# Opening of the first block: modulation rows in pairs with two projection chunks tile by tile, and the input's products with its root on VectorE

## The reference

```python
mod = jax.nn.silu(c) @ ada_w[0] + ada_b[0]                    # 6 * 1024 numbers
sh_a, sc_a, g_a, sh_f, sc_f, g_f = jnp.split(mod[:, None, :], 6, axis=-1)
h = rms_norm(x, attn_norm[0]) * (1.0 + sc_a) + sh_a           # 256 x 1024
y = sparse_mixer(h, ...)     # begins with h @ sp_w_in: 1024 x (3*512 + 512 + 768 + 24)
x = x + g_a * y
```

## Time and profile before

| | |
|---|---|
| median of 3 runs | 2203.2 us (2202.68 to 2203.76) |
| profiled execution, its own time | 2204.52 us |
| span of the profiled execution | 2202.7 us |
| granted TensorE clock, mean over the span | 0.996 of full |
| PE busy | 2156.7 us (98%) |
| DVE busy | 1847.5 us (84%) |
| ACT busy | 1327.0 us (60%) |
| HBM read | 630.13 MB, 287 GB/s over the span |

### The profile page before, as it was taken

How to read it: one execution, slowest core, us unless ns; L and a number is a source line. 1 busy time by engine, 2 the same in 40 slices (tenths; PEclk the granted TensorE clock), 3 DMA queues, 4 the chain that set the end, 5 groups by cost and what they waited for, 6 DMA issues and landing times.

```text
span 2202.7 us, 31747 instructions
## 1 busy us (share of the span) xinstructions
PE 2156.7 (98%) x12960; PEld 1899.7 (86%) x12960; DVE 1847.5 (84%) x2321; ACT 1327.0 (60%) x1495; POOL 112.2 (5%) x155
## 2 busy tenths in 40 slices
PE   6999999999999999999999999999999999999998
PEld 4888999889999979999888888888888888888886
DVE  7967888876998677888896988989897988989896
ACT  3574433575343776434633777777777777777775
POOL 3000111000010000100000000000000000000021
PEclk9999999999999999999999999999999999999999
DMA  9855988625887616885643899999998999999992
GB/s 370 299 190 201 344 314 316 230 77 211 305 299 276 225 39 239 325 325 179 227 171 136 325 372 370 365 345 363 370 358 343 369 365 371 368 345 357 373 360 85
DMA packets 137360, 633.30 MB, mean 288 GB/s; under 512 B 9304, under 2 KB 21625, under 8 KB 115194
## 3 DMA queue, kind: packets, MB, share of 16 engines
q1 hardware_dynamic: 112698, 536.83, 64.9%
q0 software_dynamic: 24512, 94.38, 11.4%
HBM read 630.13 MB, written 1.05 MB: 287 GB/s over the span
## 4 chain that ended last, share of the span: by engine, by line
PE 82%; DVE 12%; DMA 3%; issue 2%; ACT 1%; SPq 0%; DVEq 0%; ACTq 0%
PE ps L1266 80%; DVE wring_rounded L3211 3%; DMA aring<-in_ada_rows 3%; DVE aring L3238 2%; DVE work L3211 1%; PE ps L2391 1%; DVE OT L3235 1%; PE ps L1469 1%; DVE F L3218 1%; DVE F L3211 0%; PE ps L1444 0%; DVE work L3750 0%; ACT scr_rounded L2472 0%; ACT F_rounded L2472 0%; DVE work_rounded L3211 0%
## 5 line engine op out<-in xcount | busy, mean ns | idle before, releaser
L3211 DVE TENSOR_TENSOR wring_rounded<-wring,scr_rounded 128x2048 fp32r<-128x2048 f32 (+1 forms) x314 | 569.6, 1845 | 58.2 <-ACT scr_rounded L2472 57.8
L2472 ACT ACTIVATE scr_rounded<-wring 128x2048 fp32r<-128x2048 f32 (+1 forms) x314 | 479.7, 1553 | 181.8 <-PE ps L1266 125.3
L1266 PE MATMUL ps<-wring_rounded,OT_rounded 128*128 128x512 f32 (+1 forms) x1184 | 314.8, 390 | 2.6 <-DVE wring_rounded L3211 1.7
L1266 PEld LDWEIGHTS ps<-wring_rounded,OT_rounded 128*128 128x128 f32 x1184 | 220.1, 188 | 47.2 <-DVE wring_rounded L3211 2.3
L3238 DVE CUSTOM_DVE_ANT_0 aring<-aring,F,vec 128x1024 f32<-128x1024 f32 x152 | 187.9, 1283 | 35.6 <-DMA aring<-in_ada_rows 34.8
L3211 DVE TENSOR_TENSOR wring_rounded<-wring,H_rounded 128x2048 fp32r<-128x2048 f32 (+1 forms) x85 | 193.9, 2281 | 24.2 <-ACT H_rounded L2472 24.0
L3211 DVE TENSOR_TENSOR wring_rounded<-wring,aring_rounded 128x2048 fp32r<-128x2048 f32 x84 | 193.4, 2302 | 12.4 <-ACT aring_rounded L2472 12.1
L2472 ACT ACTIVATE H_rounded<-wring 128x2048 fp32r<-128x2048 f32 (+1 forms) x85 | 162.3, 1910 | 54.7 <-issue 38.4
L2472 ACT ACTIVATE aring_rounded<-wring 128x2048 fp32r<-128x2048 f32 x84 | 161.2, 1919 | 54.4 <-PE ps L1266 54.4
L1266 PE MATMUL ps<-V_rounded,wring_rounded 128*128 128x256 f32 x1184 | 177.9, 285 | 4.6 <-DVE wring_rounded L3211 4.6
L1266 PE MATMUL ps<-work_rounded,F_rounded 128*128 128x256 f32 x1056 | 169.8, 283 | 0.0
(11 more groups left out here) (391 smaller groups left out, 3695.8 us busy)
## 6 DMA issues: line engine op xcount, KB each, us to landing
wring<-in_moe_gate SPq DMA_DIRECT2D x56, 2048.0 KB, 8.5
wring<-in_moe_up SPq DMA_DIRECT2D x56, 2048.0 KB, 9.0
wring<-in_moe_down SPq DMA_DIRECT2D x56, 2048.0 KB, 8.6
aring<-in_ada_rows POOLq DMA_DIRECT2D x88, 1024.0 KB, 7.5
wring<-in_ffn_w_gate SPq DMA_DIRECT2D x10, 2048.0 KB, 11.0
wring<-in_ffn_w_up SPq DMA_DIRECT2D x10, 2048.0 KB, 15.3
wring<-in_ffn_w_down SPq DMA_DIRECT2D x10, 2048.0 KB, 10.5
wring<-in_diff_w_in SPq DMA_DIRECT2D x6, 2048.0 KB, 15.3
```

The costliest lines, as they stand in the source:

```text
L1266: return pe.matmul(dst, lhsT, rhs, start=start, stop=stop, **kw)
L2472: return act.activation(dst, src, ACT.Copy, **kw)
L3211: return ve.tensor_tensor(dst, x, y, op)
```

## The change

- The modulation rows are loaded by pairs: load k has the 128 rows of the shift for tile k and the 128 rows of the scale for the same tile. `vec`, the tables and X come ahead of them. Between load k and k+1 stand tile k of the chunks 2048:2560 and 1536:2048, 256 KB each. Load 6 goes to a buffer that load 0 had and waits for it.
- DVE makes X * root as a product of its own (`root_tile`; the root is first copied from PSUM by ACT), and ACT multiplies by gsc and adds the shift, twice: once rounded to `OTupper`, once to H. DVE then subtracts the one from the other (`lower_tile`) and makes the rests of two weight slices per tile (`slice_rest`).
- PE multiplies tile by tile for both chunks at once, with six empty products ahead of each tile (12 matmuls of 512 columns a tile, 96 in all), in the banks 0, 1, 4 and 5.
- The order behind it is 2560, 0, 512, 1024; the queries of the first two chunks are rotated and turned first. `add_more(0)` and (1) stand where (2) and (3) stood, and (2) to (5) at the end. The chunk 0:512 now has the banks 6 and 7, which `hid_job` and `kvc_job` use after it.

The diff, cut to its core; in the parts of ACT and DVE behind the opening, lines taken out are not shown.

```diff
-        sp_w = [Chunk(ring) for _ in range(5)]
+        sp_w = [Chunk(ring, dmas=0 if j < 2 else 1) for j in range(5)]
...
-        sp_tok = [[J(2 * (j % 2) + qt) for qt in range(2)] for j in range(6)]
+        sp_tok = [[J(b + qt) for qt in range(2)] for b in (0, 4, 2, 6, 0, 2)]
...
+            o = ((n + 1) % 2 if n < DF_PARTS else n % 2) * 2048
+            return buf[:, o:o + 2048]
...
+            first_rows = a["ada_rows"][0, 0:2 * D, :].rearrange("(s t p) k -> p t s k", s=2, p=P)
+            w = a["sp_w_in"][0]
...
+                if n == 6:
+                    sp.wait_ge(ada_used, 1)
+                sp.dma_start(ada0_buffer(n), first_rows[:, n]).then_inc(ada0_loaded[n], 16)
+            def load_slices(k, loaded):
+                for j, lo in enumerate((2048, 1536)):
+                    sp.dma_start(slice_weights(j, k, False), w[k * P:(k + 1) * P, lo:lo + CH]).then_inc(loaded, 16)
+            sp.dma_start(vec[:], a["vec"]).then_inc(vec_loaded, 16)
+            load_first(0)
+            for k in range(1, KT):
+                load_slices(k - 1, ada0_loaded[k])
+                load_first(k)
+            load_slices(KT - 1, last_slice_loaded)
...
-            for j, lo, n in ((1, 2560, 280), (2, 1536, 512), (3, 0, 512), (4, 512, 512)):
+            for j, lo, n in ((2, 2560, 280), (3, 0, 512), (4, 512, 512)):
...
-            pe.wait_ge(ada_used, 7)
-            idle_products(3, 14)
-            by_token_split(sp_w[0], 0, sp_tok[0], CH, OTupper, Hlower, HI_TILES[0])
+            idle_products(3, 12)
+            for job in sp_tok[0] + sp_tok[1]:
+                job.open(pe)
+            def slice_products(k):
+                def run(x, lower, last):
+                    for j in range(2):
+                        wk = slice_weights(j, k) if lower else slice_part(j, k)
+                        for qt, job in enumerate(sp_tok[j]):
+                            ins = mm(PS[job.b][:, :], x[:, k, qt * P:(qt + 1) * P], wk,
+                                     k == 0 and x is OTupper and not lower, last and k == KT - 1)
+                            if last and k == KT - 1:
+                                fill(job, ins)
+                    return ins
+                idle_products(3, 6)
+                pe.wait_ge(hi_tile, k + 1)
+                pe.wait_ge(slice_upper, 2 * k + 2)
+                run(OTupper, False, False)
+                pe.wait_ge(slice_lower, 2 * k + 2)
+                run(OTupper, True, False)
+                pe.wait_ge(lo_tile, k + 1)
+                ins = run(Hlower, False, True)
+                if k < KT - 1:
+                    ins.then_inc(slice_used, 1)
+            pe.sem_inc(part_used, 3)
+            for k in range(KT):
+                slice_products(k)
+            pe.sem_inc(part_used, 1)
             pe.wait_ge(con_loaded, 16)
-            by_token_split(sp_w[1], 2, sp_tok[1], 280, OTupper, Hlower)
-            by_token_split(sp_w[2], 4, sp_tok[2], CH, OTupper, Hlower, None, lambda: turn_rows(sp_turn[1], 2))
+            by_token_split(sp_w[2], 4, sp_tok[2], 280, OTupper, Hlower)
+            turn_rows(sp_turn[1], 0)
...
+            copy(rstd[:], PS[norm_spread[0].b][:, 0:T]).then_inc(norm_spread[0].bank.free, 1)
+            act.sem_inc(part_upper_made, 4)
+            def shifted_tile(k):
+                act.wait_ge(scaled, k + 1)
+                act.wait_ge(by_root, k + 1)
+                scale, shift = gsc[:, k:k + 1], mod[:, 0, k:k + 1]
+                affine(OTupper[:, k, :], H[:, k, :], scale, shift).then_inc(hi_tile, 1)
+                affine(H[:, k, :], H[:, k, :], scale, shift).then_inc(x_shifted, 1)
+            def round_slices(k):
+                slice_loaded(act, k)
+                if k >= 2:
+                    act.wait_ge(slice_used, k - 1)
+                for j in range(2):
+                    copy(slice_part(j, k), slice_weights(j, k, False)).then_inc(slice_upper, 1)
+            for k in range(KT):
+                shifted_tile(k)
+                round_slices(k)
+            round_part(sp_w[2], 4, 280)
             act.wait_ge(con_loaded, 16)
+            sp_tok[1][1].filled(act)
+            round_part(sp_w[2], 5, 280)
+            row_squares(sp_tok[1], 8)
+            row_roots(0, 8)
...
             row_squares(sp_tok[0], 8)
+            round_part(sp_w[3], 6)
             for qt, job in enumerate(sp_tok[0]):
+                sp_turn[1][qt].filled(act)
                 copy(work[:, 1152 + qt * 512:1280 + qt * 512], PS[job.b][:, P:2 * P])
                 copy(V[:, qt * 1024 + 512:qt * 1024 + 640], PS[job.b][:, 3 * P:4 * P])
+            row_roots(2, 8)
+            turned_rows(sp_turn[1], (F[:, 8:12, :], vc("nsa_q_rest")), (other_queries[:, 4:8, :], vc("nsa_q_rest", 1)))
+            round_part(sp_w[3], 7)
+            row_squares(sp_tok[2], 2)
+            for qt, job in enumerate(sp_tok[2]):
                 copy(V[:, qt * 1024 + 640:qt * 1024 + 768], PS[job.b][:, P:2 * P])
                 copy(gates[:, qt, :], PS[job.b][:, 256:280])
+            row_roots(4, 2)
+            round_part(sp_w[4], 8)
+            for qt, job in enumerate(sp_turn[2]):
                 job.filled(act)
                 for m, (t, k) in enumerate(((12, 0), (15, None), (13, 1), (14, 2))):
                     dst, src = F[:, t, qt * P:(qt + 1) * P], PS[job.b][:, m * P:(m + 1) * P]
                     last = copy(dst, src) if k is None else act.activation(dst, src, ACT.Identity, scale=vc("nsa_k_rest", k))
                 last.then_inc(job.bank.free, 1)
+            sp_turn[2][1].emptied(act)
             for par in range(2):
                 for g in range(2):
                     for half in range(2):
                         last = copy(*window(par, g, half, 1))
             last.then_inc(windows_ready, 1)
             row_squares(sp_tok[3], 8)
+            round_part(sp_w[4], 9)
             row_roots(6, 8)
+            round_part(sp_w[5], 10)
...
+                w, o = ada0_buffer(n), VEC["ada_b"][0] + n
+                for m in range(2):
+                    last = ve.tensor_tensor_reduce(w[:, m, :], w[:, m, :], crow, 1.0, vec[:, o + KT * m:o + KT * m + 1],
+                                                   ALU.mult, ALU.add, mod[:, 0, n + KT * m:n + KT * m + 1])
+                last.then_inc(ada_used, 1)
+            def root_tile(k):
+                tt(H[:, k, :], X[:, k, :], rstd[:], ALU.mult).then_inc(by_root, 1)
+            def scale_tile(k):
+                ve.wait_ge(ada_used, k + 1)
+                o = VEC["attn_norm"][0] + k
+                stt(gsc[:, k:k + 1], mod[:, 0, KT + k:KT + k + 1], 1.0, vec[:, o:o + 1], ALU.add, ALU.mult).then_inc(scaled, 1)
+            def slice_rest(j, k):
+                ve.wait_ge(slice_upper, 2 * k + j + 1)
+                tt(slice_weights(j, k), slice_weights(j, k, False), slice_part(j, k).bitcast(F32), ALU.subtract).then_inc(
+                    slice_lower, 1)
+            def lower_tile(k):
+                ve.wait_ge(x_shifted, k + 1)
+                tt(Hlower[:, k, :], H[:, k, :], OTupper[:, k, :].bitcast(F32), ALU.subtract).then_inc(lo_tile, 1)
...
+            ve.sem_inc(part_lower_made, 4)
+            for job in crow_job:
+                job.emptied(ve)
+            add_first(0)
+            scale_tile(0)
+            for k in range(1, KT):
+                add_first(k)
+                if k == 1:
+                    inverse(0)
+                    norm_spread[0].emptied(ve)
+                    root_tile(0)
+                scale_tile(k)
+                root_tile(k)
+                lower_tile(k - 1)
+                for j in range(2):
+                    slice_rest(j, k - 1)
+            lower_tile(KT - 1)
+            for j in range(2):
+                slice_rest(j, KT - 1)
+            part_rest(sp_w[2], 4, 280)
+            part_rest(sp_w[2], 5, 280)
             ve.wait_ge(rotary_made, 4)
             ve.wait_ge(con_loaded, 16)
+            row_sums(0, 8)
+            rows(0, sp_tok[1], 8, ((0, 0, 8, 4),), None)
             def rests(j):
                 for n in (2 * j + 3, 2 * j + 4):
                     if n < 12:
+                        part_rest(sp_w[n // 2], n)
+            row_sums(2, 8)
+            part_rest(sp_w[3], 6)
+            rows(2, sp_tok[0], 8, ((0, 0, 2, 5), (4, 4, 2, 6)), sp_turn[1])
+            part_rest(sp_w[3], 7)
+            row_sums(4, 2)
+            rows(4, sp_tok[2], 2, ((0, 6, 2, 7),), None)
+            part_rest(sp_w[4], 8)
+            sp_turn[2][1].emptied(ve)
...
-            add_more(2)
+            add_more(0)
...
-            add_more(3)
+            add_more(1)
...
-            for n in range(4, 6):
+            for n in range(2, 6):
```

More of the change, by code:

```diff
@@ L711, in build @@
         for M, tag in ((moe2, "again"),):
-            for name in ("upper", "lower", "gathered", "sel", "wsel", "xg", "st", "silu", "hid", "ht", "ye", "acc"):
+            for name in ("upper", "lower", "gathered", "sel", "wsel", "hid"):
                 M[name] = sem(f"{tag}_{name}")
```

(34 more changed lines are left out.)

77 lines of the change are left out of this document (16 added, 61 removed).

## The result

The changed kernel takes 2216.4 us (median of four runs, 2215.88 to 2219.15) against 2203.5 (2202.68 to 2204.01) for the kernel before beside it: 1.0062 times as long, interval 1.0044 to 1.0079. It is slower, by 13 us where I forecast 2.6, and outside my range. The profiled execution took 2215.88 us, its span 2214.0 against 2202.7.

A forecast was written before the change was run, and what follows sets the result against it. The prediction took the kernel to be bound by PE (82% of the chain), with DVE's late work deciding: compressed_scores at 124.1 against 121.55, so 2.6 us later, 2205.8 us against 2203.2. The range was 2200 to 2211.

The forecast's parts named there:

- The first pair: Opening: load 1 and the slices 0 end a queue of 4.3 MB and are usable at 15.2 us.
- DVE's beat: Opening's stream: DVE needs 4.6 us per tile against 3.9 for the loads, so it sets the pace.
- PE in the stream: Opening: PE needs 4.05 us a tile, is the later one at the last, and ends the stream at 55.9.
- DVE's list: From 57.1 us to the compressed keys' signal: 55.9 us of work plus 5.6 of waits, giving 118.6.
- The new wait: End of DVE's work before the signal: 3.1 us of waiting for the load of add_more(4).
- The sum: Signal at 118.6 plus 5.5 us puts compressed_scores at 124.1 against 121.55, so 2.6 us later; chance .64.
- The clock: Rival, in the opening's stream: waits drop PE to 1.2 GHz, 7.8 us a tile; three low tiles give about 2214; chance .11.
- PE's clock at 1.00 behind 24 us: Sign of a right forecast: in the trace after, PE's granted clock is full from 24 us on.
- a memset before 114, a stream's end past 59: Signs of a wrong forecast: DVE's memset before 114 us (then PE decides), or the opening's stream ending past 59.
- The faster one: Rival: stream follows the loads, ends at 51.9, late loads land in time; 4.6 us gained, 2198.6; chance .14.
- The third: Rival, opening's stream: loads at 300 GB/s take 5.2 us a tile, stream ends 4 us later, 2210; chance .11.
- PE's list alone: From 55.9 us to compressed_scores: PE by itself would get there at 120.9, a gain of .7 us.

The follow-up runs named there:

- warm_units: The changed kernel with 12 empty products on PE ahead of its wait for the compressed keys and 10 behind unit 2's scores: 2210.2 us, ratio 1.0036.
- before_moved_warm: The kernel before with its six additions moved late as in the change, plus 12 and 10 empty products on PE: 2207.7 us, ratio 1.0016.
- stream_no_empties: The changed kernel without the six empty products ahead of each tile in the opening's stream: 2211.6 us, ratio 1.0040.
- gaps_no_empties: The changed kernel with add_more(4) and (5) moved to units 1 and 3 and the stream's empty products left out: 2203.0 us, ratio 1.0003.
- adds_in_gaps: The changed kernel with add_more(4) and (5) moved ahead of the row maxima of units 1 and 3: 2205.6 us, ratio 1.0021.
- before_two_in_units: The kernel before with add_more(6) and (7) moved ahead of the row maxima of units 1 and 10: 2206.3 us, ratio 1.0009.
- before_adds_moved: The kernel before with only its six add_more moved to the places the change gives them: 2214.6 us, ratio 1.0045.
- product_with_scale: The changed kernel with DVE's product per tile taking the scale again and ACT adding only the shift: 2219.0 us, ratio 1.0064.
- adds_in_units: The changed kernel with add_more(4) and (5) moved ahead of the row maxima of units 3 and 4: 2210.4 us, ratio 1.0029.
- load_apart: The changed kernel with the second half of the output weights loaded only once add_more(3)'s load has landed: 2215.8 us, ratio 1.0053.

## Why the prediction was wrong

**The first pair, DVE's beat, PE in the stream: right.** 16.76 for 15.2, 4.48 for 4.6, 57.1 for 55.9. The 1.6 us at the start are the pair's own landing, which ends DVE's wait at 16.76. X was late too (PE's sums for the norm end at 17.8, not 15.0) but stayed covered by the two additions. The shorter beat gave back 0.7.

**DVE's list: right in kind, 3.2 us short.** The term that was too small is the wait for loads. DVE takes the list up at 58.55 for 57.1, which is 1.4. The new wait, which I saw in one place (3.1 us ahead of `add_more(4)`), is three: 1.42, 1.70 and 1.61, 4.73 in all. I had the load for (4) issued 0.3 behind (2) and landing 5.25 later; a load in that stretch takes 5.2 us alone and 10.5 beside 2 MB of weights. The work of 55.9 us was right within 1 us: from 58.55 to the memset's signal are 63.3 us, and the forecast 61.5 plus the 1.6 of waits is 63.1; the waits for ACT were 0.6 less than forecast, the work that much more. The Trainium skill's figure for such a load ("DMA: Bandwidth & Descriptors", "Anatomy of one DMA — SWDGE (gpsimd) path"), by which I estimated 4.4 us, would have made this worse, by 0.8 us; the measured 5.2 decides, and the 10.5 is in neither.

**The sum: the step that failed.** I carried the signal's lateness to `compressed_scores` and from there to the end, as a plain delay: 118.6 + 5.5. The clock had a place in my reckoning, but in the stream, as a rival at .11. Behind the signal, where PE was to stand still and wait for a list that I had just shown to be late, I gave it no price, and named "PE's clock at 1.00 behind 24 us" among the signs of a right forecast. There it cost 6.3 us (`warm_units`; 5.4 to 7.3 by the ways to take it) in the changed kernel, and 5.9 to 6.9 with the old opening (`before_moved_warm`). Without the clock's share the plain delay holds: `warm_units` is 5.7 us over its own before, and 2.6 forecast plus 3.2 of the list is 5.8. A forecast with both would have been 2205.8 + 6.3 + 3.2 = 2215.3; the 1.1 us left of the 2216.4 is about what the medians of before differ by between the two batches. Neither sign that I had set down for being wrong (a memset before 114, a stream's end past 59) came up, since both look at DVE's list and the stream alone.

**The rivals.** The faster one fell with the loads: DVE's list decides. The clock was the right mechanism at the wrong place, and that the time it named (2214 for three low tiles) is near the measured one is chance. The stream keeps its clock, even with PE idle a third of the round (`stream_no_empties`). So what the Trainium skill tells of a kernel that waits for each weight slice ("TensorE: Matmul & The Clock Gate", "HAM oscillation — how this bites in real kernels") does not come about in this stream, where PE is idle 1.46 us of 4.48; the waits that the page shows are longer. Behind the stop of 2.42 us ahead of the units there is such a fall. The third, slow loads in the stream, did not happen: no wait for DMA from 24 us on, at 368 to 402 GB/s.

**Where the gain is.** `gaps_no_empties` says what the change is worth with its by-effects removed: 0, within 0.2%. The forecast of PE's list alone, 0.7 us earlier at the first compressed scores, was for a stream with its empty products. The kernel to hold beside it is `adds_in_gaps`, where PE's list decides: 122.38, 0.8 later than before, with a stream that ends 1.75 late (57.65 for 55.9). Without the empty products it is 0.5 earlier (121.03 against 121.55), which the norm (200.72 against 200.63) no longer has. In the opening DVE's 4.5 us per tile set the pace, and in the changed kernel its list behind it too.

## What to carry to other kernels

Lateness of an engine is not yet a price. When the forecast says that TensorE will wait for a late list, put two terms down: the wait, and the work behind it at the lower clock; here the second was no smaller than the first (6.3 us and 5.7). Work that is moved to the end of an engine's list should go to a measured idle time of that engine instead, one instruction group at a time. A group of 2.4 us in a gap of 0.8 (unit 10 in `before_two_in_units`) shows up again as a stop of the engine that feeds on it. And before cutting a piece of the chain, look at what ends beside it: here 27.89 us of matmuls.

## What the runs showed of the hardware

- TensorE kept its full granted clock (1.00) through five rounds of 4.48 us in which it was idle for 1.43 to 1.47 us each (`stream_no_empties`). In the changed kernel the clock fell to 0.50 at 123.5 us, 1.6 us after a stop of 2.42 had ended and before the second one began. With the old opening (`before_adds_moved`) it fell at 123.4, just behind a stop of 2.00 us that followed one of 0.94.
- How long it stays low differs, though TensorE has work all the while: from the end of its last stop to the rise it worked 8 us in the changed kernel (125.7 to 133.7), and 17 in `before_adds_moved` (123.2 to 140.1) and `product_with_scale` (126.2 to 143). What decides this is open.
- A single stop of 1.97 us was followed by a fall in one kernel (`adds_in_units`, 0.52 from 132 to 134 us), and one of 1.98 by none in another (`before_two_in_units`). What differed is open.
- Empty products in the changed kernel's two stops, 12 and 10 of 512 columns, kept the clock at 1.00 and made the median 6.3 us lower (7.3 each beside its own before).
- A modulation load of 1 MB took 5.2 us alone (`load_apart`) and 10.5 beside a weight load of 2 MB issued 0.3 us ahead of it (the changed kernel).
